# Which buffer a late weight load takes, and how many unread products fill the last step

## What is computed

```python
def swiglu(x, wg, wu, wd):
    return (jax.nn.silu(x @ wg) * (x @ wu)) @ wd
...
    def expert_block(args):
        xi, e = args
        return swiglu(xi, p['exp_w_gate'][e], p['exp_w_up'][e], p['exp_w_down'][e])

    yb = lax.map(expert_block, (xb, block_e)).reshape(n_blocks * MOE_BLK, D)
    routed = jax.ops.segment_sum(yb[dest] * w_s[:, None], tok_s, num_segments=T)
    shared = swiglu(xf, p['sh_w_gate'], p['sh_w_up'], p['sh_w_down'])
    return (routed + shared).reshape(B, N, D)
```

## Time and profile before

| | us |
|---|---|
| median of 3 runs | 1273.56 |
| lowest, highest | 1272.36, 1274.42 |
| the profiled execution, whole | 1273.56 |
| its span in the profile | 1271.7 |

### The profile page before, as it was taken

The page is one execution under the profiler, slowest core; times in us unless marked ns, Lnnn a source line. Parts: engine busy times, 40 slices in busy tenths (PEclk is TensorE's granted clock), DMA queues, the critical chain, the costliest instruction groups (busy, mean ns, idle before and its releaser), DMA issues.

```text
span 1271.7 us, 22864 instructions
## 1 busy us (share of the span) xinstructions
PE 1206.7 (95%) x9511; PEld 801.3 (63%) x9511; DVE 310.6 (24%) x883; ACT 192.9 (15%) x471; POOL 37.8 (3%) x73
## 2 busy tenths in 40 slices
PE   8999999998999999978999999999899999999696
PEld 4445776664677667655554568767467676776363
DVE  2047442213111111111030764321311111111012
ACT  1125221100111111010010452111011101110011
POOL 2210000000000000000020100000000000000000
PEclk9999999998999999998999999999899999999799
DMA  9999998999999999989995896999999999999995
GB/s 367 401 349 403 405 387 356 411 419 422 420 421 420 416 420 421 420 366 420 409 384 217 329 375 241 400 367 419 420 421 421 420 420 419 421 421 376 423 420 200
DMA packets 86630, 495.00 MB, mean 389 GB/s; under 512 B 11948, under 2 KB 18016, under 8 KB 33024
## 3 DMA queue, kind: packets, MB, share of 16 engines
q1 hardware_dynamic: 83744, 488.38, 94.5%
q0 software_dynamic: 2240, 4.64, 1.1%
q10 hardware_dynamic: 544, 0.52, 0.1%
HBM read 491.20 MB, written 2.50 MB: 388 GB/s over the span
## 4 chain that ended last, share of the span: by engine, by line
PE 67%; issue 24%; DVE 4%; DMA 3%; ACT 1%; SPq 1%; POOL 0%; POOLq 0%; ACTq 0%; DVEq 0%
PE ps L1393 16%; PE ps L1330 9%; PE ps L1352 8%; PE ps L1428 8%; PE ps L931 7%; PE ps L1159 4%; PE ps L898 3%; PE ps L1283 3%; DMA ring<-in_exp_w_up 2%; DMA ring<-in_w_ada 1%; PE ps L1116 1%; PE ps L1141 1%; PE ps L1124 1%; DVE ht L1701 1%; PE ps L916 1%
## 5 line engine op out<-in xcount | busy, mean ns | idle before, releaser
L1393 PE MATMUL ps<-ring,kt_buf 128*32 128x256 f32 (+2 forms) x3200 | 308.3, 393 | 22.3 <-DMA ring<-in_exp_w_gate 12.4
L1393 PEld LDWEIGHTS ps<-ring,kt_buf 128*32 128x32 f32 (+2 forms) x3200 | 188.3, 124 | 133.1 <-issue 55.7
L1330 PE MATMUL ps<-kt_buf,attn 128*128 128x128 f32 x1472 | 179.7, 275 | 3.6 <-DVE kt_buf L2023 1.8
L1330 PEld LDWEIGHTS ps<-kt_buf,attn 128*128 128x128 f32 x1472 | 175.0, 192 | 8.5 <-issue 4.3
L1352 PE MATMUL ps<-kt_buf 128*128 128x256 f32 x704 | 163.8, 385 | 3.2 <-DVE kt_buf L2141 1.8
L1352 PEld LDWEIGHTS ps<-kt_buf 128*128 128x128 f32 x704 | 130.3, 190 | 38.1 <-issue 15.2
L1428 PE MATMUL ps<-ring,kt_buf 128*32 128x512 f32 (+1 forms) x544 | 133.6, 598 | 0.7 <-DMA ring<-in_exp_w_down 0.7
L931 PE MATMUL ps<-ring,ht 128*128 128x456 f32 x256 | 98.9, 547 | 0.3 <-DVE ht L1701 0.3
L1628 ACT ACTIVATE kt_buf<-ps 128x512 f32<-128x512 f32 x44 | 26.3, 598 | 419.5 <-PE ps L1410 419.5
L2058 DVE COPY kt_buf<-ps 128x512 f32<-128x512 f32 x46 | 31.8, 691 | 219.3 <-PE ps L1330 219.3
L931 PEld LDWEIGHTS ps<-ring,ht 128*128 128x128 f32 x256 | 48.3, 190 | 50.6 <-issue 48.2
(11 more groups left out here) (307 smaller groups left out, 1152.9 us busy)
## 6 DMA issues: line engine op xcount, KB each, us to landing
ring<-in_exp_w_up SPq DMA_DIRECT2D x104, 1024.0 KB, 19.5
ring<-in_exp_w_gate SPq DMA_DIRECT2D x96, 1024.0 KB, 18.5
ring<-in_exp_w_down SPq DMA_DIRECT2D x68, 1024.0 KB, 17.0
ring<-in_w_ada SPq DMA_DIRECT2D x10, 3072.0 KB, 13.5
spare<-in_exp_w_up SPq DMA_DIRECT2D x16, 1024.0 KB, 26.2
spare<-in_exp_w_down SPq DMA_DIRECT2D x16, 1024.0 KB, 23.3
attn<-in_exp_w_down SPq DMA_DIRECT2D x14, 1024.0 KB, 14.9
spare<-in_exp_w_gate SPq DMA_DIRECT2D x12, 1024.0 KB, 9.2
```

Of the source, the lines that this page charges most:

```text
L1330: last = pe.matmul(ps[:, 4 + b, (c % 4) * P:(c % 4 + 1) * P], h2[:, t, c * P:(c + 1) * P], pick[:, t, :], start=(t == 0), stop=(t == NG - 1))
L1393: last = pe.matmul(ps[w * e:w * (e + 1), b, 0:DE], xg[:, k, w * e:w * (e + 1)], half_of(chunk_of(l, load_of(part, i, e)))[:, k, :], start= ...
```

## The change

Three numbers change and nothing else. The rule for the last rounds now holds for the last four rounds (loads 124 to 191) and not two, it asks for content that is 13 loads old and not nine, and the last step of each layer has two unread products and not five.

```diff
-WARM_LAST = 5
+WARM_LAST = 2
...
-LONG_SPENT = 9
+LONG_SPENT = 13
+LAST_ROUNDS = 4
...
-        elif turn < 2:
+        elif turn < LAST_ROUNDS:
             unused = [c for c in range(NCH) if holds[c] < len(LOADS) - (turn + 1) * NCH]
             p = min((c for c in unused if holds[c] <= n - LONG_SPENT), key=next_layer.index)
```

## The result

| | before | changed |
|---|---|---|
| median of the runs, us | 1273.56 (1272.36 to 1274.42, 5 runs) | 1267.49 (1265.68 to 1267.95, 5 runs) |
| ratio | | 0.9953 (95%: 0.9940 to 0.9966) |
| span of the profiled execution, us | 1271.7 | 1266.0 |

The account below looks back on a forecast made before the run. Loads were taken to bound the kernel, with a hole in their stream. Closing it and dropping three unread products gave 4.6 us in layer 0 and 4.3 in layer 1: 1273.56 - 8.9 = 1264.7 us, range 1262.0 to 1267.5.

Parts of the forecast that it names:

- The bound and its cause: Mixture stages: loads set the pace; loads 159 to 161, at distance 9, wait for step 17's gate and empty the queue.
- How long the hole is: Load stream between landings of loads 158 and 187: 3.3 us lost in layer 0, 2.4 in layer 1.
- The prediction's own sign of being wrong: Step 20, layer 0: the forecast is wrong if the up load lands less than 3 us earlier.
- The unread products: Before step 20's up products: five take 4.39 us a layer; dropping three gives at most 2.63 while the load stays.
- The second bound: Last step's down products wait for second weight halves, landing at 634.3 in layer 0; gains limited to 4.6 and 4.3 us.
- Layer 0's gain reaches the end: Layer 1's first needed load lands at 641.7, is read at 642.4; layer 0's gain holds by 0.7 us.
- Waits of step 18: TensorE's waits before gate and up become about 3 and 6 us, where they were 6.18 and 4.19.
- The clock: Behind step 18's waits TensorE may fall to 1.2 GHz again; term bounded by 0 to 1.3 us, taken as 0.
- rival 1: The lower clock behind step 18's waits takes part of the gain, 1.3 us: 1266.0 us; chance 0.08.
- Rival 2: The hole in the load stream counts by bytes, 4.1 and 3.2 us: gain 10.5, 1263.1 us; chance 0.08.
- Rivals 3 and 4: Hole stays or moves, only unread products act: 1270.3, chance 0.05; layers' last step at 1.2 GHz: 1289, chance 0.03.
- Rival 4: Layers' last step at 1.2 GHz, TensorE busy 12 of 15 us: up to 12 us each, 1289; chance 0.03.

Follow-up runs that it names:

- unread0: Changed kernel with no unread product in each layer's last step where it has two: 1268.66 us, ratio 0.9970 to the kernel before.
- side3_new: Changed kernel plus, in each layer, an unread 17-row transfer of 0.21 MB ahead of step 12's loads: 1271.93 us, ratio 0.9991 to the kernel before.
- side2_new: Changed kernel plus, in each layer, an unread 17-row transfer of 0.14 MB ahead of step 12's loads: 1265.99 us, ratio 0.9955 to the kernel before.
- unread1: Changed kernel with one unread product in each layer's last step where it has two: 1267.39 us, ratio 0.9962 to the kernel before.

## Why the prediction was wrong in size, step by step

- *The bound and its cause*: right. The hole was where the queue's row had it, the distance of 13 and more closed it, and no new dip came between 456 and 530 (419 to 422 GB/s in slices 15 to 17).
- *How long the hole is*: this step failed. The prediction let TensorE have 3.3 and 2.4 us, as 29 loads of 2.49 us from the last landing of load 158. For the new kernel that assumes that the last part keeps its distance from the mean from 158 on. Layer 0: from 3.3 the slower pace takes 0.4 (29 loads took 72.6 by the mean, not 72.2), the larger lag 0.9 (3.38 at load 187, against 2.46 at load 158 of the kernel before), and 0.2 is scatter of load 158's mean; 1.8 are left, and 1.73 were measured. Layer 1: 2.4 - 0.4 - 1.1 (lag 3.56) = 0.9, and 0.9 was measured. The lag is 2.0 us of the 3.1 that are missing, the pace 0.8. The sentence "TensorE waits for landings, so I take 3.3 and 2.4" had the right reason. But the landing of the new stream has to be worked out with the lag of a stream that runs without a stop. The prediction's own sign of being wrong, a load 187 less than 3 us earlier in layer 0, came true. The amount of this lag is measured; why it grows beyond 2.46 is open, see below.
- *The unread products*: right. TensorE was ready before the load in the changed kernel (wait 0.96 and 0.98, forecast 0.3 to 1.1). In layer 1 the sum had 0.3: there the load's gain came 1.5 us short and TensorE's only 0.9.
- *The second bound*, the halves of the down weights: right as a mechanism, wait 0.41 in layer 0, 636.0 instead of 634.3, for the same reason as load 187.
- *Layer 0's gain reaches the end*: right, in this kernel's trace. No TensorE wait for a DMA in the first part of layer 1, and the weight stream there is 2.7 us earlier.
- *Waits of step 18*: forecast 3 and 6, measured 4.62 and 4.79. Load 165 came only 2.0 us earlier, again by its last part, so the gate products kept most of their wait.
- *The clock* (rival 1): it does fall behind both waits of step 18, to 0.50 from 569.8 to 573.2 and from 580.1 to 583.5, and this ends long before step 20 starts; the load sets the start, and the term is 0 as taken. The example of the Trainium skill that the prediction names (TensorE: Matmul & The Clock Gate, section HAM oscillation) has waits of 3 to 5 us. Here waits of 2.6 us were followed by a fall (unread0), and those of 1.8 and 1.0 us for the same load were not.
- *Rival 2*, the hole by bytes: right for the mean of the parts (4.1 and 3.2), and of no use, since nothing waits for the mean. *Rivals 3 and 4* did not come. Rival 4's 12 of 15 us is too low by its own source: 17.73 of 20 makes 13.3 of 15. Nothing else hangs on it.

What stays open is what makes a part fall behind. In the traces the lag grows by 0.9 to 1.4 us from one load to the next, for example at load 151 of layer 0 in the changed kernel, and at load 175 or 176 of layer 1 in six of the nine traces of the new table, but in none of the old one nor in side3_new, where another part is 4.7 us late. Near such places lies one of the 76 packets of 16 KB of the instruction queue, which take 1.07 us of one engine (median), where a packet of a load takes 0.31. That would fit, but no run moved or removed them, so it isn't shown. Nor was a kernel tried that closes the hole and lets the parts meet in another way.

## What to carry to other kernels

When you remove a gap from a stream of loads, cost it by the last part of the load that somebody waits for, in the new stream. The gap was also where late parts caught up, and about 2 us of its 3 to 4 came back as lag (1.3 us at load 187 with the gap, 2.6 to 3.9 without). Two edits that move the two sides of one wait have to be costed together and tested together: alone they gave 2.8 and 0.8 us, together 5.4 to 6.1. Follow the gain past the wait as well, since a fall of the clock far behind it can take it away. Unread products paid here only as far as the wait that they leave did not take the clock down: one was enough, and five were in the way.

## What the runs showed of the hardware

- The sixteen parts of a 1 MB load don't land together. In a stream at 421 GB/s the last one was 1.4 to 3.5 us behind the mean between loads 100 and 158 in the nine traces without an added transfer, and 2.6 to 3.9 at load 187 in those of the new table. A pause of the stream of some 4 us brought a lag of 5.90 down to 2.14 us.
- A transfer of 17 rows went on one engine: 0.2 MB took 8.5 us of it, and cost the kernel 4.4 us. The Trainium skill (DMA: Bandwidth & Descriptors, section Why a DMA increments its semaphore by 16 and not by 1) says that the number of engines is the largest divisor of the row count up to 16, which is one for 17 rows. The trace agrees: 17 packets, one behind the other.
- A part that is late gains on the others slowly: in side3_new the lag went from 6.60 at load 111 to 5.27 at load 187, 1.3 us in 190. In side2_new 3.72 at load 111 became 2.84 at load 158.
- The granted clock fell to 1.2 GHz behind a wait of 2.6 us for load 187 and did not behind one of 1.8. That is no rule for other places: in unread1 it fell at 790.2, behind four short groups of products and waits of 0.61 and 0.87 us, and in eleven other traces it did not fall there.
